# Eight row buffers in place of seven, eleven held weight chunks in place of twelve, in a two-layer decoder trunk

## What is computed

```python
def hybrid_layer(x, ...):
    h = rmsnorm(x, g_mix)
    z = h @ w_in                                   # 1024 -> 4096: p, q, k, v, gate logits
    branch_a = pool_mixer(p, w_pool, pool_scale)
    o = moba_attention(q, k, v)                    # 256 tokens are one block: causal attention with ALiBi
    branch_b = o @ w_attn_up
    merged = gates[..., :D] * branch_a + gates[..., D:] * branch_b
    x = x + merged @ w_out
    x = x + peer_ffn(rmsnorm(x, g_ffn), w_peer_q, peer_keys, peer_u, peer_v)

def peer_ffn(x, ...):                              # 8 heads, 16 of 16384 experts for each head and token
    q = x @ w_q                                    # 1024 -> 2048
    eid, g = top 16 of (top 16 + top 16) of q @ keys, softmax
    act = gelu(sum_d(u[eid] * x))
    y = sum over 128 picked experts of (g * act) * v[eid]
```

## Time and profile before

| what | value |
|---|---|
| median of 3 runs | 1549.62 us (1547.36 to 1549.95) |
| profiled execution, its time | 1548.52 us |
| its span, first to last instruction | 1546.7 us |
| busy: TensorE, VectorE, ScalarE, GpSimd | 1274.5, 1136.4, 913.0, 661.5 us |
| moved by DMA | 643.51 MB, a mean of 416 GB/s |

### The profile page before, as it was taken

How to read it: one execution, slowest core, us unless ns; L and a number is a source line. 1 busy time by engine, 2 the same in 40 slices (tenths; PEclk the granted TensorE clock), 3 DMA queues, 4 the chain that set the end, 5 groups by cost and what they waited for, 6 DMA issues and landing times.

```text
span 1546.7 us, 18716 instructions
## 1 busy us (share of the span) xinstructions
PE 1274.5 (82%) x5582; PEld 783.1 (51%) x5582; DVE 1136.4 (73%) x2598; ACT 913.0 (59%) x3311; POOL 661.5 (43%) x520
## 2 busy tenths in 40 slices
PE   8999898876998788756688978797878987788886
PEld 8986566542554465533355546564545532232322
DVE  2159998877888769536788886976778777777555
ACT  2226566567667446434676664655676666666776
POOL 0014344455445333323544542334654555554554
PEclk9999999988899899987799999999989999999999
DMA  9989999999999999999999999999999999999998
GB/s 393 400 335 405 408 413 426 426 427 427 424 421 404 426 427 426 426 426 427 426 414 424 402 427 427 421 426 426 423 426 405 426 427 428 426 427 426 427 411 328
DMA packets 90317, 643.51 MB, mean 416 GB/s; under 512 B 10040, under 2 KB 10600, under 8 KB 12904
## 3 DMA queue, kind: packets, MB, share of 16 engines
q0 software_dynamic: 74304, 536.90, 83.1%
q1 hardware_dynamic: 15588, 105.18, 16.3%
q10 hardware_dynamic: 324, 0.23, 0.0%
HBM read 641.23 MB, written 1.05 MB: 415 GB/s over the span
## 4 chain that ended last, share of the span: by engine, by line
DMA 42%; PE 27%; DVE 17%; ACT 6%; issue 5%; POOL 2%; DVEq 0%; POOLq 0%; ACTq 0%
DMA ring<-in_uv,expert 41%; PE ybank L691 15%; PE bank L486 8%; DVE ring L1208 6%; DVE xs L1221 3%; POOL ring L1372 2%; ACT diag L910 2%; ACT wgt L900 1%; DMA wring<-in_chunks 1%; PE bank L632 1%; ACT th L898 1%; PE bank L621 1%; PE bank L464 1%; DVE si L945 1%; DVE buf L939 1%
## 5 line engine op out<-in xcount | busy, mean ns | idle before, releaser
L1372 POOL DMA_INDIRECT ring<-in_uv,expert x508 | 651.4, 1282 | 867.7 <-PE ybank L691 528.0
L691 PE MATMUL ybank<-ring,diag 128*128 128x512 f32 x1528 | 785.1, 646 | 248.2 <-ACT diag L910 247.2
L1208 DVE SCALAR_TENSOR_TENSOR ring<-ring,tok 128x1024 f32<-128x1024 f32 x512 | 624.3, 1224 | 299.4 <-DMA ring<-in_uv,expert 295.1
L691 PEld LDWEIGHTS ybank<-ring,diag 128*128 128x128 f32 x1528 | 278.9, 199 | 627.4 <-ACT diag L910 403.8
L892 ACT ACTIVATE sq<-dots 128x1 f32<-128x1 f32 x512 | 102.5, 200 | 490.1 <-DVE ring L1208 488.7
L900 ACT ACTIVATE wgt<-th,half_p 128x1 f32<-128x1 f32 x512 | 198.1, 387 | 17.1
L486 PEld LDWEIGHTS bank<-hT,wring 128*128 128x128 f32 x1536 | 185.5, 198 | 34.5 <-issue 30.1
L486 PE MATMUL bank<-hT,wring 128*128 128x128 f32 x1536 | 186.6, 281 | 8.1 <-DMA wring<-in_chunks 7.8
L1221 DVE SCALAR_TENSOR_TENSOR xs<-ring,wgt,xs 128x1024 f32<-128x1024 f32 x128 | 164.0, 1281 | 5.3 <-ACT wgt L900 3.7
L910 ACT ACTIVATE diag<-cst,wgt 128x128 f32<-128x128 f32 x384 | 154.2, 402 | 12.4
L898 ACT ACTIVATE th<-arg,dots 128x1 f32<-128x1 f32 x512 | 150.8, 295 | 16.6
(11 more groups left out here) (143 smaller groups left out, 790.3 us busy)
## 6 DMA issues: line engine op xcount, KB each, us to landing
wring<-in_chunks SPq DMA_DIRECT2D x52, 1024.0 KB, 9.4
held<-in_chunks SPq DMA_DIRECT2D x24, 1024.0 KB, 24.8
ring<-in_chunks SPq DMA_DIRECT2D x20, 1024.0 KB, 12.3
ring<-in_uv,expert POOLq DMA_INDIRECT x508, 11.5
xs<-in_x SPq DMA_DIRECT2D x2, 512.0 KB, 4.4
wpool<-in_w_pool SPq DMA_DIRECT2D x2, 512.0 KB, 13.3
trunk_out<-buf SPq DMA_DIRECT2D x4, 256.0 KB, 4.9
ring<-in_pool_scale SPq DMA_DIRECT2D x1, 512.0 KB, 14.8
```

The lines of the kernel that those rows point to most:

```text
L691: ins = pe.matmul(ybank[m][:, :], diag[:, nth % DIAGS, :], ring[:, (2 * t + r) % RING, D + m * BANK:D + (m + 1) * BANK], start=(nth == ten ...
L1208: dve.scalar_tensor_tensor(out=ring[:, g % RING, 0:D], in0=ring[:, g % RING, 0:D], scalar=1.0, in1=tok[:, :], op0=ALU.mult, op1=ALU.mult, ...
L1372: pool.indirect_dma_start(ring[:, g % RING, :], None, uv, bass.IndirectOffsetOnAxis(ap=expert[:, at:at + 1], axis=0)).then_inc(row_landed[ ...
```

## The change

One row buffer is added and one held buffer is given up, so the memory taken stays the same. Query chunk 27 (head 5) becomes a slot chunk: every tile loads it anew, and in the first tile it takes the first slot. Chunk 29 (head 7) is then third in the first tile's slot order and has to wait for the use of chunk 27; its load is moved behind the loads of `NEXT_CHUNKS` and the spread, so that they don't stand in the queue behind this wait. The early chunks go through seven row buffers in place of six.

```diff
-HELD = 12
+HELD = 11
...
-RING = 7
+RING = 8
...
                     for c in range(CHUNKS):
                         if tile == 0 and layer and c == 0:
                             heads(layer)
-                        if w != 1 or c not in NEXT_CHUNKS:
+
+                        if (w != 1 or c not in NEXT_CHUNKS) and (w or slot_turns.get((w, c), 0) < W_SLOTS):
                             chunk(w, c)
...
                         sp.dma_start(tok[:, :], spread).then_inc(gain_spread, 16)
+                        for n in range(W_SLOTS, len(slot_order)):
+                            if slot_order[n][0] == 0:
+                                chunk(*slot_order[n])
```

## The result

The changed kernel takes 1551.91 us (median of 18 runs, 1551.12 to 1552.74), beside 1548.75 us for the kernel before on the same chip: a ratio of 1.0020, 95% interval 1.0013 to 1.0026. It is slower by 3.2 us. The forecast was 1543.4, and the time lies above the range as well.

A forecast was written before the change was run, and what follows sets the result against it. The prediction took DMA bytes at 426 GB/s plus idle DMA time as the limit from the first gather on. Its sum, +7.4 us for bytes less 13.6 for the buffer, gave -6.2: 1543.4 us, range 1540.5 to 1551.5.

The forecast's parts named there:

- What bounds the kernel: From the first gather on, time is bytes at 426 GB/s plus 16.8 us in which DMA had too little to do.
- shortfall: Per stretch of the profile, length x (1 - rate/426), taken as DMA time lost; 16.8 us over all stretches.
- Bytes, +7.4 us: Behind the first gather, four slot loads more and one held load less: three chunks net at 2.46 us each.
- The eighth buffer, -13.6 us: In each stretch with idle DMA, one more queued row gives back up to 2.46 us; 13.6 us in all.
- the first dip: At 102 to 130 us, DMA 4.4 us short; the added buffer was to give back up to 2.46 us.
- The later dips: Stretches of lower DMA rate from 400 to 1500 us, credited 2.46, 1.1, 2.2, 1.8 and 1.1 us.
- Chunk 29 in time: In the first tile, its later load lands at 164.1 us, 3.8 us before TensorE wants it at 167.9.
- The start, nothing: Ahead of the first gather, seven early-chunk buffers cost nothing, since TensorE sets that stretch; its 5.2 us not busy bound a gain.
- The first: Rival: stretches after 200 us don't refill the lead, some 40% of 9.8 us come back; 1548.2 us, chance 0.26.
- The second and the third: Rivals: chunks land late, 1558 us at half, chance 0.09; the queue holds no more rows, 1557.0 us, chance 0.03.
- The sum's own far end: Only the two stretches up to 200 us give back time: +7.4 - 4.9 = +2.5 us, 1552.1 us.
- What would show it: Rates at 183 to 200, 850 to 872 and 1184 to 1204 us rise from 363, 383, 387 to above 410 GB/s.

The follow-up runs named there:

- the first experiment: The changed kernel with seven row buffers in place of eight, held chunks and the moved chunk 29 load kept: 1554.06 us, ratio 1.0039 to the kernel before.

## Why the prediction was wrong, point by point

*What bounds the kernel.* Right that it is the transfers, at 2.45 us a row. Wrong in how it was measured: I took the shortfall of the *mean* over 16 engines for time in which the stream stands still. The dip at 1184 to 1204 us, priced at 1.8 us, shows the error. Landing of the last part (us), gap to the row before, and the first part's lead, from the traces:

```
row       368    369    370    371    372    373    374    375    376    377    378
before 1182.9 1185.4 1187.9 1190.3 1192.9 1195.4 1197.9 1200.7 1203.2 1206.2 1208.6
gap             2.44   2.47   2.44   2.56   2.54   2.46   2.88   2.43   3.02   2.43
lead      3.1    3.1    3.2    3.2    3.3    3.2    1.2    1.7    1.4    2.0    1.9
after  1182.9 1185.3 1187.8 1190.2 1192.7 1195.2 1197.8 1200.4 1202.8 1206.3 1208.7
gap             2.47   2.45   2.44   2.49   2.48   2.60   2.57   2.44   3.44   2.43
lead      6.1    5.9    5.9    5.8    5.9    5.9    5.3    4.7    4.3    5.3    5.3
```

In before, eight gaps to row 376 make 20.2 us in place of 8 x 2.45 = 19.6: 0.6 us late, while the mean says 1.8. The mean fell because engines with a lead of 3.1 us spent it: at row 376 it is 1.4. After, the rows are 0.3 us late, but so they are with seven buffers in the first experiment (0.4), and at row 378 before and after are level. All later dips that were priced in full, and the last one, by how much the last part of the rows named falls behind 2.45 us a row (shortfall: the mean's, from the prediction):

```
stretch      shortfall          rows       before   seven, chunks as after   after
400-500            2.6          101-139     3.06     4.40 (with a chunk)     4.25 (with a chunk)
776-794            1.1          221-230     0.04    -0.06                   -0.06
850-872            2.2          251-259     0.70     2.47 (with a chunk)     2.47 (with a chunk)
1184-1204          1.8          368-376     0.64     0.38                    0.35
1482-1500          1.4          487-493     2.23     2.24                    2.24
```

So three of the five dips are in the main a lead that is spent, 1.4 us late where 5.1 were priced. In the other two the last part does fall behind, by 3.1 and 2.2 us (rows 70 to 100, without a dip, by 0.8), and still seven and eight buffers come out alike. Between 1482 and 1500 us SyncE's first output stores pass, 0.52 MB of packets from 1484.7 to 1491.2 us, which fits; at 400 to 500 us the cause is open.

A row has landed with the last of its 16 parts, and in the traces they come one by one: 16 updates of the semaphore for each row, 2.9 us from the first to the last in the median of before. After, the median row has two late parts, 1.2 us apart, and fourteen that come 3.5 us ahead of the last or more. The trace does not name the engines, and no run here shows which of them are late.

*Bytes, +7.4 us.* Right in the main: +1.66, +2.11 and +2.60 us at three added loads, -2.27 at the saved one. As a whole, with seven buffers, the first experiment puts them at 5.5 us: the moved chunk 29 may have cost less than its 2.46 (1.3 in its own run), and the load at 457 us, in a dip, 1.66.

*The eighth buffer, -13.6 us.* This is the step that failed: "each dip gives back the smaller of its shortfall and 2.46 us". Measured, the buffer is worth 1.9 to 2.4 us: one lead, won once, in the first dip, which was priced about right. The second, at 183 to 200 us, was priced at another 2.46, though the prediction itself has VectorE as the limit from 102 to 200 us: the lead of row 8 was not spent before it, and at row 64 the rows are 2.5 us ahead of those with seven buffers, not 4.9. The later dips, 8.7 us in the sum, gave 0.1: 3.06 us at row 64, with the 0.6 of the start in it, and 3.19 at row 480. (Against before, rows 64 to 496 lose 4.2 us with seven buffers and 4.45 with eight, so none of the 0.5 won there against the bytes is the buffer's.) The premise that the buffers refill in saturated stretches is right (the landing rose by a row), but what refills is the lead of engines that were ahead already. Put together from runs: 5.5 us for the chunks (first experiment) less 1.9 for the buffer (without chunk 27) are 3.6, beside the 3.2 found.

*Chunk 29 in time.* Right. SyncE issues it at 154.49 us, it has landed at 163.5, and TensorE uses it at 167.33 with no wait:

```profile
154.49 0.33 SPq L1407 DMA_DIRECT2D wring<-in_chunks  x1
```

```profile
167.33 3.74 PE L486 MATMUL bank<-hT,wring 128*128 128x128 f32 x32
```

*The start, nothing.* Right: the first gather is 0.15 us later. To 102 us TensorE is busy for 96.82 us with DMA at 380 GB/s, and for 96.70 at 370 GB/s after, so TensorE and not the loads sets that stretch in both. The first row of before lands at 106.3 us, 5.6 after its gather went out at 100.77.

*The rivals.* The first let 40% of the later dips come back (1548.2); it was too mild. (What it held against itself, DMA at 99 to 100%, is 0.98 at 776 to 794 us.) The second and the third did not happen, as TensorE's waits and the landing show. The sum's own far end, "with the start's two dips alone: +2.5", was the nearest to the 3.2 us found, in part by luck: it takes the start's one lead for two (4.9 for 1.9 to 2.4) and pays the chunks in full (7.4 for 5.5), and the two errors nearly cancel. It stood as the far end of the first rival's case, and the range was cut at 1551.5, short of it.

*What would show it.* Rising rates in three stretches were to confirm the forecast. Two rose and confirmed nothing: an added or moved chunk load fills a dip of the mean just as an earlier row would. The landing of a given row, before and after, tells the two apart.

*Faster than both kernels?* Only the two that leave chunk 27 out were, and they compute something else. Seven buffers stand just past the knee: six cost 42 us, nine bring nothing.

## What to carry to other kernels

A mean over 16 DMA engines at 99% does not say that the transfer someone waits for could come sooner; look at when the last part of it lands, and at whether those landings keep their pace through the dip (1184 to 1204 us: 1.8 us short by the mean, 0.6 late at the landings). The worth of one more buffer in a ring is read from the trace before it is built: count the rows whose time from landing to release exceeds n times the pace less the bare landing. Here that count placed the knee, though not the time at which the buffer pays. Where few are left (22 of 501 here), what the buffer displaces weighs more: 5.5 us for the chunks against 1.9 to 2.4 for the buffer. And a lead counts once: here it was not spent between two stalls, and the second added nothing.

## What had not been expected of the hardware

- 0.25 MB on one DMA engine cost 9.35 us; 0.26 MB spread evenly cost 0.85.
- A load of 119 x 8 KB over seven engines made the 8 KB packets of all engines take 0.51 us in place of 0.31, for 17 us; the load of 32 x 8 KB over 16 engines did likewise for some 2 us (0.50 us, 282 GB/s). The load of 31 x 8 KB on one engine did not (0.31 us), nor do the kernel's own loads of 128 x 8 KB (0.309 in the trace of before). Why was not tried.
- The page's DMA queues carry code as well: 44 packets of 16 KB of instructions in the trace of before took about 0.94 us each, three times a row's packet of 8 KB (0.309). What they cost the rows was not tried.
- The ring's knee is sharp: +168, +42, +2 and 0 us for the sixth, seventh, eighth and ninth buffer.
